# Two stacked transformer blocks on one core: a smaller share of the modulation on TensorE, and branch products in three fp32r passes

## What is computed

```python
# per layer of the second block
mod = silu(c) @ w_ada + b_ada                    # 1024 -> 9*1024, for c and c_ctx
x = x + HALF * gate1 * swiglu(ada_norm(x, g_ffn1, shift1, scale1), w1, w3, w2)   # 2816 wide
u = ada_norm(x, g_mix, shiftm, scalem)
y_conv = silu(layer_norm(conv(...))) @ w_pw_conv + b_pw        # 384 -> 1024
y_four = real(fft2(...)) @ w_fourier + b_fourier               # 512 -> 1024
y_mla  = attention(...) @ w_o_mla                              # 512 -> 1024
g = sigmoid(u @ w_bgate + b_bgate)                             # 1024 -> 3*1024
x = x + gatem * ((g0 * y_conv + g1 * y_mla + g2 * y_four) @ w_out)
x = x + HALF * gate2 * swiglu(ada_norm(x, g_ffn2, shift2, scale2), w1, w3, w2)
```

## Time and profile before

| | before |
|---|---|
| median of 3 runs, us | 2916.12 (2908.54 to 2918.16) |
| the profiled execution, us | 2909.88 |
| its span, us | 2908.1 |
| its mean granted TensorE clock | 0.989 |
| TensorE busy, of the span | 2814.7 us, 97% |
| TensorE weight load | 2343.8 us, 81% |
| VectorE | 1646.7 us, 57% |
| ScalarE | 1123.8 us, 39% |
| GpSimd | 46.8 us, 2% |
| DMA traffic, mean | 138 GB/s |

### The profile page before, as it was taken

How to read it: one execution, slowest core, us unless ns; L and a number is a source line. 1 busy time by engine, 2 the same in 40 slices (tenths; PEclk the granted TensorE clock), 3 DMA queues, 4 the chain that set the end, 5 groups by cost and what they waited for, 6 DMA issues and landing times.

```text
span 2908.1 us, 44638 instructions
## 1 busy us (share of the span) xinstructions
PE 2814.7 (97%) x16512; PEld 2343.8 (81%) x16512; DVE 1646.7 (57%) x2847; ACT 1123.8 (39%) x1723; POOL 46.8 (2%) x36
## 2 busy tenths in 40 slices
PE   8999999999999999999999999999999999899998
PEld 7659999569988888775666778888788887688998
DVE  7457656566665565586334576555533336645665
ACT  5345544345442221335544232222322214584443
POOL 0000000000000000030000000000000000000000
PEclk9999999999999999999999999999999999999999
DMA  5565554665544434321221333443222223234454
GB/s 189 204 223 174 181 172 158 242 217 198 181 145 152 144 138 135 117 77 51 71 69 55 101 123 138 151 139 129 94 101 94 96 95 110 78 114 144 166 183 154
DMA packets 118357, 400.08 MB, mean 138 GB/s; under 512 B 12896, under 2 KB 20960, under 8 KB 117856
## 3 DMA queue, kind: packets, MB, share of 16 engines
q1 hardware_dynamic: 115120, 391.43, 39.8%
q10 hardware_dynamic: 3120, 7.07, 0.7%
HBM read 397.40 MB, written 1.05 MB: 137 GB/s over the span
## 4 chain that ended last, share of the span: by engine, by line
PE 86%; DVE 5%; DMA 3%; ACT 2%; issue 2%; DVEq 1%; POOL 1%; SPq 0%; ACTq 0%; POOLq 0%
PE bank L820 23%; PE bank L827 23%; PE bank L824 23%; PE bank L2294 4%; DMA ring<-weights 3%; PE bank L1553 2%; PE bank L2003 1%; PE bank L1983 1%; DVE w_lo L781 1%; PE bank L1475 1%; PE bank L918 1%; PE bank L1477 1%; PE bank L1482 1%; DVE work L2072 1%; PE bank L1295 1%
## 5 line engine op out<-in xcount | busy, mean ns | idle before, releaser
L781 DVE TENSOR_TENSOR w_lo<-ring,w_hi 128x1024 fp32r<-128x1024 f32 (+1 forms) x538 | 649.2, 1208 | 681.9 <-ACT w_hi L757 679.3
L757 ACT ACTIVATE w_hi<-ring 128x1024 fp32r<-128x1024 f32 (+1 forms) x548 | 571.6, 1044 | 1156.9 <-DMA ring<-weights 1156.4
L824 PE MATMUL bank<-hn_hi,w_hi 128*128 128x256 f32 (+1 forms) x2816 | 883.7, 334 | 0.0
L827 PE MATMUL bank<-hn_lo,w_hi 128*128 128x256 f32 (+1 forms) x2816 | 883.5, 333 | 0.0
L824 PEld LDWEIGHTS bank<-hn_hi,w_hi 128*128 128x128 f32 x2816 | 535.5, 190 | 52.2
L827 PEld LDWEIGHTS bank<-hn_lo,w_hi 128*128 128x128 f32 x2816 | 535.5, 190 | 52.1
L820 PE MATMUL bank<-hn_hi,w_lo 128*128 128x256 f32 (+1 forms) x2816 | 555.9, 340 | 9.6 <-DVE w_lo L781 6.5
L820 PEld LDWEIGHTS bank<-hn_hi,w_lo 128*128 128x128 f32 x2816 | 443.2, 190 | 78.6 <-issue 19.1
L824 PE MATMUL bank<-hid_hi,w_hi 128*128 128x512 f32 (+1 forms) x704 | 248.7, 362 | 0.0
L827 PE MATMUL bank<-hid_lo_a,w_hi 128*128 128x512 f32 (+1 forms) x640 | 226.2, 362 | 0.0
L820 PE MATMUL bank<-hid_hi,w_lo 128*128 128x512 f32 (+1 forms) x704 | 156.4, 362 | 0.0
(11 more groups left out here) (325 smaller groups left out, 2969.6 us busy)
## 6 DMA issues: line engine op xcount, KB each, us to landing
ring<-weights SPq DMA_DIRECT2D x692, 512.0 KB, 3.3
ring<-weights SPq DMA_DIRECT2D x32, 384.0 KB, 3.0
ring<-weights SPq DMA_DIRECT2D x32, 256.0 KB, 2.6
ring<-weights SPq DMA_DIRECT2D x28, 192.0 KB, 2.3
con<-consts ACTq DMA_DIRECT2D x1, 2063.0 KB, 9.7
con<-consts ACTq DMA_DIRECT2D x1, 1088.0 KB, 4.9
res<-ctx_cm ACTq DMA_DIRECT2D x1, 1024.0 KB, 5.6
con<-params ACTq DMA_DIRECT2D x1, 1024.0 KB, 7.3
```

The costliest lines, as they stand in the source:

```text
L757: act.activation(w_hi[:, slot, 0:w], ring[slot][:, 0:w], ACT.Copy).then_inc(s.w_hi, 1)
L781: eng.tensor_tensor(w_lo[slot][:, 0:w], ring[slot][:, 0:w], w_hi[:, slot, 0:w].bitcast(F32), ALU.subtract).then_inc(s.w_lo, 1)
L824: pe.matmul(dst, high, x_hi(k), start=False, stop=False)
L827: return pe.matmul(dst, high, x_lo(k), start=False, stop=(stop and k == order[-1]))
```

## The change

It has two parts.

- **The modulation.** `ADA_TICKS` keeps 40 of the 84 chunks (10 quads) on TensorE in the first block's attention. The other 104 tiles are rows for VectorE. They ride in `ffn1`, `ffn1_out`, `ffn2`, `ffn2_out` of layer 0 as before, and now also in `mrg_conv` and `mrg_four` of layer 0 and `ffn1` and `ffn1_out` of layer 1: 106 row chunks, two of them a repeat of the last. Short VectorE instructions at stage ends (`rows_ready`) add the bias and form the gains.
- **The branch products.** They become three fp32r passes and stand behind the gate's product of their group. GpSimd makes `w_hi` and `w_lo` of the branch's weights (`branch_weights`, signalled by `branch_w`) and of the three branches' operands (`source_split`). VectorE takes the branch's result once the slot of the branch is released. TensorE's waits for `ln_out` and for the last `att_o` are gone, and ScalarE's first split for `mrg_conv` moves ahead of the other copies of V.

```diff
-ADA_TICKS = ([2, 2, 2, 2, 2, 2, 0, 4, 0, 0, 4, 0, 0, 4, 0, 4, 0, 4, 0, 4, 0, 4, 0, 0, 0, 0, 0, 0],
-             [2, 2, 2, 2, 2, 2, 0, 4, 0, 0, 4, 0, 0, 4, 0, 4, 0, 4, 0, 4, 0, 4, 0, 4, 0, 0, 0, 0])
+ADA_TICKS = ([2, 2, 2, 2, 2, 2, 0, 4, 0, 0, 4] + [0] * 17,) * 2
...
-ADA_QUADS = (5, 5, 6, 5)
+ADA_QUADS = (3, 2, 3, 2)
...
+ALL_ROWS = 72 * DEPTH
+ROWS_AT, ROW_STAGES = {}, (("ffn1", 0, FF2), ("ffn1_out", 0, KT), ("mrg_conv", 0, KT), ("mrg_four", 0, KT),
+                           ("ffn2", 0, FF2), ("ffn2_out", 0, KT), ("ffn1", 1, FF2),
+                           ("ffn1_out", 1, KT))
+for name, l, n in ROW_STAGES:
+    ROWS_AT[name, l] = sum(ADA_CHUNKS) + sum(x[2] for x in ROW_STAGES[:len(ROWS_AT)])
+assert ROWS_AT["ffn1_out", 1] + KT - 2 == ALL_ROWS
...
-         ("ffn1", 1): (2, 1), ("ffn1_out", 1): (2, 1), ("conv_in", 1): (3, 0), ("ffn2", 1): (3, 1),
+         ("ffn1", 1): (2, 0), ("conv_in", 1): (2, 0), ("ffn2", 1): (3, 1),
...
-        order += [("ffn1", l, FF2, (8, 8) + rows, (0, 1)), ("ffn1_out", l, 8, (8, 8, 6) + rows, (0, 1, 2)),
+        order += [("ffn1", l, FF2, (8, 8, 8), (0, 1)), ("ffn1_out", l, 8, (8, 8, 6, 8), (0, 1, 2)),
                   ("conv_in", l, CT, (8, 8), (0, 1)), ("lat_in", l, 10, (8,), (0,)),
                   ("uq", l, Q_TILES, (3,), ()), ("uk", l, QH // 2, (2,), ()), ("uv", l, 1, (8,), ()),
-                  ("mrg_conv", l, 8, (3, 8), (1,)), ("mrg_four", l, 8, (4, 8), (1,)), ("mrg_mla", l, 8, (4, 8), (1,)),
+                  ("mrg_conv", l, 8, (3, 8) + rows, (1,)), ("mrg_four", l, 8, (4, 8) + rows, (1,)),
+                  ("mrg_mla", l, 8, (4, 8), (1,)),
...
+        own = {"in_a": 1, "ffn1": 2, "ffn1_out": 3, "ffn2": 2, "ffn2_out": 3, "mrg_conv": 2,
+               "mrg_four": 2}.get(name, len(tiles))
...
+        def source_hi(b, k):
+            if b == 0:
+                return means_r[:, k, :] if k < 2 else hid_hi[:, 21, :]
+            if b == 1:
+                return hid_hi[:, (4, 5, 18, 19)[k], :]
+            return hid_hi[:, 6 + k, :]
+        def source_lo(b, k):
+            return hid_hi[:, (18, 6, 0)[b] + k, :]
...
         def branch_pe(pe, l, b, g):
             name, kt, _ = BRANCHES[b]
             w = seqs(l) * T
             lin = PLAN[name, l]
+            wait_banks(pe, lin, g)
+            input_product(pe, lin, g, 1, bank[2 * parity(lin, g) + 1][:, 0:w], 2 * DEPTH + 3 * l + 1, w)
+            slot, dst = slot_of(lin, g, 0), bank[2 * parity(lin, g)][:, 0:w]
+            pe.wait_ge(s.branch_w, g.m + (KT * (3 * l + b) + 1))
+            for k in range(kt):
+                if g.at == 0:
+                    pe.wait_ge(s.source_hi, source_rows(l, b) + k + 1)
+                pe.matmul(dst, w_lo[slot][:, k * P:(k + 1) * P], source_hi(b, k)[:, 0:w], start=(k == 0), stop=False)
+            for k in range(kt):
+                high = w_hi[:, slot, k * P:(k + 1) * P]
+                pe.matmul(dst, high, source_hi(b, k)[:, 0:w], start=False, stop=False)
+                if g.at == 0:
+                    pe.wait_ge(s.source_lo, source_rows(l, b) + k + 1)
+                mm = pe.matmul(dst, high, source_lo(b, k)[:, 0:w], start=False, stop=(k == kt - 1))
+            mm.then_inc(used[slot], 1)
...
+        def branch_weights(pool, l, b, m):
+            lin = PLAN[BRANCHES[b][0], l]
+            g, w = Group(m, m, 0, period(lin.cpg)), BRANCHES[b][1] * P
+            slot = slot_of(lin, g, 0)
+            wait_weights(pool, lin, g, 0)
+            pool.tensor_copy(w_hi[:, slot, 0:w], ring[slot][:, 0:w])
+            pool.drain()
+            pool.tensor_tensor(w_lo[slot][:, 0:w], ring[slot][:, 0:w], w_hi[:, slot, 0:w].bitcast(F32),
+                               ALU.subtract).then_inc(s.branch_w, 1)
...
+        def source_split(pool, b, ks, w):
+            for k in ks:
+                source_high(pool, b, k, 0, w).then_inc(s.source_hi, 1)
+            pool.drain()
+            for k in ks:
+                source_low(pool, b, k, 0, w).then_inc(s.source_lo, 1)
...
+            if lin.cpg > lin.own:
+                row_dot(dve, lin, g, 2, row_of(BRANCHES[b][0], l, g.m))
             splits_ahead(split_low, dve, lin, g, after_branch(l, b))
             dve.wait_ge(s.sig_g, g.m + (KT * (3 * l + b) + 1))
+            dve.wait_ge(used[slot_of(lin, g, 0)], turn_of(lin, g, 0) + 1)
...
-            pe.wait_ge(s.ln_out, l + 1)
...
-            pe.wait_ge(s.att_o, units[-1].o + 1)
...
+                    if tt == 0:
+                        first_split(split_high, act, PLAN["mrg_conv", l])
             units = units_block2(l)
-            first_split(split_high, act, PLAN["mrg_conv", l])
...
+                    branches_pool(pool, l)
```

More of the change, by code:

```diff
@@ L371, in pairs, with put_row, merging @@
             put(y[m])
+    def put_row(name, l, m):
+        if (name, l) in ROWS_AT:
+            put(rows[min(ROWS_AT[name, l] + m, ALL_ROWS - 1)])
+    def merging(name, l, x, gate):
+        for m in range(KT):
+            put(x[m])
+            put(gate[m])
+            put_row(name, l, m)
     ada = [t for l in range(DEPTH) for t in quads(a["w_ada_2"][l])]
-    rows = a["w_ada_2"][1].T.reshape(ROW_TILES, P, 8, P)
+    rows = np.concatenate([a["w_ada_2"][l].T.reshape(72, P, 8, P) for l in range(DEPTH)], 0)
     for l in range(DEPTH):
@@ L404, in feed_forward @@
                 put(t[:, c:c + 8])
[L405 to L406 removed]
+            put_row(f"{name}_out", l, m)
     for l in range(DEPTH):
@@ L427, in pack_stream @@
         pw, four, om = (tiles(a[n][l]) for n in ("w_pw_conv_2", "w_fourier_2", "w_o_mla_2"))
-        pairs(pw, gate[0:8])
-        pairs(four, gate[16:24])
-        pairs(om, gate[8:16])
+        merging("mrg_conv", l, pw, gate[0:8])
+        merging("mrg_four", l, four, gate[16:24])
+        merging("mrg_mla", l, om, gate[8:16])
         halves(tiles(a["w_out_2"][l]), 8)
@@ new lines, in wait_branch, with branches_pool @@
+        def wait_branch(pool, l, b):
+            lin = PLAN[BRANCHES[b][0], l]
+            g = Group(KT - 1, KT - 1, 0, period(lin.cpg))
+            pool.wait_ge(used[slot_of(lin, g, 0)], turn_of(lin, g, 0) + 1)
+        def branches_pool(pool, l):
+            w = seqs(l) * T
+            units = units_block2(l)
+            branch_weights(pool, l, 0, 0)
+            pool.wait_ge(s.ln_out, l + 1)
+            source_split(pool, 0, range(CT), w)
+            branch_weights(pool, l, 0, 1)
+            pool.wait_ge(s.f_sb, fourier_steps(l)[-1][0] + 1)
+            source_split(pool, 1, (0, 1), w)
+            for m in range(2, KT):
+                branch_weights(pool, l, 0, m)
+            branch_weights(pool, l, 1, 0)
+            wait_branch(pool, l, 0)
+            source_split(pool, 1, (2, 3), w)
+            for m in range(1, KT):
+                branch_weights(pool, l, 1, m)
+            branch_weights(pool, l, 2, 0)
+            wait_branch(pool, l, 1)
+            if seqs(l) == 2:
+                pool.wait_ge(s.att_o, units[2 * QH - 1].o + 1)
+                for k in range(4):
+                    source_high(pool, 2, k, 0, T)
+                pool.drain()
+                for k in range(4):
+                    source_low(pool, 2, k, 0, T)
+            for k in range(4):
+                last = units[2 * QH + 4 + k] if seqs(l) == 2 else units[QH + 2 * k + 1]
+                pool.wait_ge(s.att_o, last.o + 1)
+                source_high(pool, 2, k, w - T, w).then_inc(s.source_hi, 1)
+                pool.drain()
+                source_low(pool, 2, k, w - T, w).then_inc(s.source_lo, 1)
+            for m in range(1, KT):
+                branch_weights(pool, l, 2, m)
@@ L2623, in block2_dve @@
                 branch_dve(dve, l, 2, g)
+            rows_ready(dve, "mrg_mla", l)
             gated_add(dve, l, PLAN["mix_out", l], 1, w, PLAN["ffn2", l],
```

111 lines of the change are left out of this document (60 added, 51 removed).

## The result

| | before | after |
|---|---|---|
| median, us | 2914.99 (4 runs) | 2975.34 (4 runs, 2970.16 to 2977.74) |
| ratio to before | | 1.021 (1.019 to 1.023) |
| profiled execution, us | 2909.88 | 2976.97 |
| its span, us | 2908.1 | 2975.2 |
| its mean granted TensorE clock | 0.989 | 0.970 |

The change makes the kernel slower by 60 us; 2954.5 was predicted, +38.4, with a range of 2918 to 2980. The forecast was added to the 2916.12 of the three runs known then. One execution of the changed kernel, in its repetition on another chip, took 12117 us at a granted clock of 0.686 and is in no ratio.

The account below looks back on a forecast made before the run. TensorE, 86% of the chain that ended last, was taken to bound the kernel. Terms −31.7 + 43.6 + 33 − 5.6 − 4.0 − 0.9 + 4.0 gave +38.4 on 2916.12: 2954.5 us, range 2918 to 2980.

Parts of the forecast that it names:

- main case: Whole kernel: all terms summed, 2954.5 us, own range 2940 to 2966, given 62%.
- dearer transfers: Rival, layer 0's merge: gate's chunk lands in 4.59, not 3.45; 15 waits grow by 1.14, +17.1, 2971.6 us; 10%.
- the move: First block's attention: 44 modulation chunks leave TensorE, −31.7 us, bounds −35.4 and −28.
- the merge: Layer 0's `mrg_conv` and `mrg_four`: 15 waits for the gate's chunk, +43.6 us, and +33 for the clock.
- That is 13.61 and 14.29: Layer 0's merge: predicted us per period in `mrg_conv` and `mrg_four`, from handover, gate, first pass after a wait and branch.
- the handover of 5.83: Layer 0's merge: us from slot release to gate's product: 3.45 to ScalarE, 1.10 to VectorE, 1.28 for its split.
- Before, this point came at 1541.11.: Layer 0's merge: time taken as the old end of the 16 groups, set against 1584.8 to give +43.6 us.
- The clock … 2.2 for each: +33: Layer 0's merge: TensorE's clock falls after each of 15 waits, 2.2 us lost each, +33; bounds +22 and +41, or nothing.
- `mrg_mla` … every second group waits 2.08 … +4.0: Layer 1's `mrg_mla`: transfers issued when branch m−1 ends make every second group wait 2.08 us; stage 40.8 against 36.8, +4.0.
- No wait, and faster: Rival, layer 0's merge: no wait or clock loss comes and the passes win there too, −48.0, 2868 us; 7%.
- The full clock stays: Rival, layer 0's merge: waits don't lower the clock, the +33 falls away, +5.4, 2921.5 us; 12%.

Follow-up runs that it names:

- second profile of the change: The change itself, unaltered, run and profiled once more on another chip: 2975.02 us against 2913.53 for the kernel before, ratio 1.021.
- filling the waits: The change with 20 added matmuls ahead of each of the 15 late gate products in layer 0's merge: 2938.24 us; with 8 matmuls, 2951.57.
- `mrg_mla` alone: The change with chunk order gate, branch in `mrg_mla` only, `mrg_conv` and `mrg_four` as in the change: 2958.47 us against 2913.72 before, ratio 1.015.

## Why the prediction was right, and where it was off

**The number** came out inside the stated range but above the main case's own, 2940 to 2966; the room made for dearer transfers holds it. The mechanism is shown, but most terms were short. Between the two profiles these are the move (6.0 less won), the merge (11.8), the rest of the attention (8.4) and `mrg_mla` of layer 1 (7.2); the other stages give back 4.6.

**The place and the mechanism** were as predicted: waits at each gate of layer 0's merge after the first, released by VectorE's split, behind a transfer that SP could only issue at the end of the branch's product. Chunk order and product order, changed one at a time, each took them away.

**"That is 13.61 and 14.29"**, the handover of 5.83 in it. It measured 6.31 on average (6.06 to 6.62), and the part up to ScalarE 3.84 (3.60 to 4.16) where I took 3.45. Rows 7 themselves have 3.56 from release to ScalarE. The part behind was right to 0.1: 1.09 to VectorE and 1.38 to the product. 0.5 us in each of 15 waits is 7 us. The first two waits were the longest, 5.16 and 4.66, since the attention has fewer pieces there to fill them; the handover is as long there (6.18 and 6.12).

**"Before, this point came at 1541.11."** This was misread. That row of rows 2 is the second unit's scores behind the last group; the last group ended at 1538.70. The stage was 171.05 us long, not 173.5, and by the right row the term would have been 1584.8 − 1538.7 = 46.1, and 53 with the longer handover. The ledger has 88.4 − 38.6 = 49.8; the 0.27 a period for the first pass after a wait (4 in all) is in the clock's share there. It is a slip of the reading and not of the mechanism.

**"The clock … 2.2 for each: +33"** measured 38.6 by the ledger, 31 in the second profile of the change, and 30 to 37 by filling the waits. So 33 was right within what executions of one kernel differ by. The argument from the length of a wait was not. The waits ahead of the second and third stretch of rows 9 were these:

```profile
847.44 0.62 PE L1475 MATMUL bank<-hn_hi,w_lo 128*128 128x512 f32 x1 [3.08 <-ACT hn_hi L1013]
...
432.63 0.36 PE L1475 MATMUL bank<-hn_hi,w_lo 128*128 128x256 f32 x1 [2.51 <-ACT hn_hi L1006]
```

The longest, 3.08, lost less (1.68) than the one of 2.60 (2.75). Later 3.62 and 3.73 kept the full clock in one turn each, and waits of 5.5 lost 2.0 a turn against 2.1 to 2.6 behind 4.0. What decides it in a given turn stays open. The Trainium skill's rule ("TensorE: Matmul & The Clock Gate", section "HAM oscillation — how this bites in real kernels"), that a loop which waits for a transfer in each turn falls to the low clock in each turn, agrees with the first profile in all 15 turns, where each gate's product took 7.04 us or more in place of 5.46, and with the second in 14 of 15. Its example's 0.83 us lost a turn does not; 2.0 to 2.6 were measured.

**"`mrg_mla` … every second group waits 2.08 … +4.0"** was right in kind (2.55, 2.73, 2.21 in every second group) and short in size, +11.2. The waits were longer by 0.4 each, which fits the longer handover above; in other executions they were spread differently, and the stage lost 6.5 to 11.2. Two further waits, 0.30 at the start and 1.47 at `mix_out`, were not in the sum, and the clock (0.93 in this stretch) I had put at nothing.

**The rest of the attention** was missing from the sum. I counted 15 waits for 16 groups and took the sixteenth chunk to be hidden behind the attention. It is not, since the engines that wait for it are those that serve the attention: +8.4, and 23.6 us again once that chunk had another slot (`mrg_mla` alone).

**"−31.7"** for the move came out as −25.7 in these two profiles, and as −31.4 by the medians of the move alone. Up to the second block's first norm, the ten profiles of kernels with the change's first block end between 818.5 and 825.6; the two with the first block of before end at 847.4 and 855.2. One profile of this stage is good to some 4 us, and no more should be read from it.

**The rivals.** "No wait, and faster" did not come, but its number, 2868, is what the kernel does once the slots are right: 2865 and 2872 were measured. "The full clock stays", 2921.5, was ruled out for the change; the filled waits show about what that case would have been, 2938, with the terms missed elsewhere in it. "The transfers are dearer", 2971.6, came near the measured time by luck: a gate's chunk did come later than a single one, by 0.4 of the 1.14 priced there, and the rest of the difference was elsewhere.

## What to carry to other kernels

- In a ring, a chunk can be issued when its own slot and those of all chunks ahead of it in the queue are free. Write down, for every chunk, which read releases its slot, whenever a group grows by a chunk or a product changes its place in the group. Here two edits, each of which won by itself (31 and 17 us), lost 60 together, and a swap of two entries in a table gave back 111.
- A wait on TensorE costs more than its length. Where waits of some 4 us recur, add what the low clock takes from the product behind; here 15 waits of 4.0 cost 2.1 to 2.6 more each, by the execution.
- Where a split is made one group ahead, look at what is queued behind it on ScalarE and VectorE at the end of the stage.
